# Mixing stage: query blocks in pairs from the middle outwards, alternating by groups of four heads

## The reference

```python
# A: memory branch (mLSTM), 16 chunks of 128 tokens, 4 heads; the state goes from chunk to chunk
(h, C, n, m) = mlstm(q, k, v, gates, chunk=128)        # a recurrence over the chunks
# B: sparse attention, 16 query blocks of 128 tokens, 8 query heads, 2 key heads (4 query heads share one)
_, sel = top_k(indexer_scores(iq, iw, ik, visible), 256)
yb = softmax(q @ k[sel].T * HD ** -0.5) @ v[sel]       # query t sees keys 0 .. t only
```

## Time and profile before

| | us |
|---|---|
| runs | 4074.53, 4076.52, 4077.44; median 4076.52 |
| span of the profiled execution | 4076.9 |
| TensorE busy | 3909.3 (96%) |
| VectorE busy | 2910.3 (71%) |
| GpSimd busy | 1670.9 (41%) |
| ScalarE busy | 1430.2 (35%) |
| mixing stage, first score matmul to last copy | 2255.0 to 3103.6 |

### The profile page before, as it was taken

One profiled execution on the slowest core, in us unless ns is written; L12 is line 12 of the kernel. 1 busy time (PEld: TensorE's weight loads), 2 busy tenths in 40 slices (PEclk: granted clock), 3 DMA queues, 4 the chain that ended last, 5 costly groups with the idle time before them and its releaser, 6 DMA issues. The chain is left out here.

```text
span 4076.9 us, 41822 instructions
## 1 busy us (share of the span) xinstructions
PE 3909.3 (96%) x14574; PEld 2311.2 (57%) x14574; DVE 2910.3 (71%) x3885; ACT 1430.2 (35%) x2616; POOL 1670.9 (41%) x1517
## 2 busy tenths in 40 slices
PE   7899999999999999999998799899999899999999
PEld 4555555563465556655665566555554688854444
DVE  4589989668999999999997555544543577753333
ACT  4411211155324443343331566545553322211111
POOL 0000036459786665566554232222202666552111
PEclk9999999999999999999999899999999899999999
DMA  5312222420111111211211643222232755541111
GB/s 217 90 53 65 64 83 84 141 89 36 59 66 64 63 60 62 69 62 68 68 63 58 179 110 103 66 84 64 78 97 73 214 168 168 169 143 60 41 57 46
DMA packets 290632, 367.34 MB, mean 90 GB/s; under 512 B 72223, under 2 KB 219187, under 8 KB 287734
## 3 DMA queue, kind: packets, MB, share of 16 engines
q1 hardware_dynamic: 250602, 249.50, 20.2%
q0 software_dynamic: 18704, 85.56, 5.7%
q10 hardware_dynamic: 21120, 29.66, 2.4%
HBM read 235.11 MB, written 128.23 MB: 89 GB/s over the span
## 5 line engine op out<-in xcount | busy, mean ns | idle before, releaser
L1274 DVE MAX8 best<-score 128x8 f32<-128x640 f32 (+13 forms) x448 | 639.6, 1428 | 60.4 <-POOL score L1235 45.4
L1276 DVE MATCH_REPLACE8 score<-best,score 128x640 f32<-128x640 f32 (+13 forms) x448 | 631.1, 1409 | 0.0
L1026 PE MATMUL pr<-xnT,w_row 128*128 128x347 f32 (+1 forms) x960 | 300.5, 459 | 0.0
L1176 POOL TENSOR_TENSOR kT<-kT 128x347 f32<-128x347 f32 (+1 forms) x240 | 194.5, 811 | 227.7 <-ACT kT L1096 221.3
L382 PE MATMUL pg<-xnT,wt 128*128 128x416 f32 x800 | 282.0, 515 | 0.0
L1642 PE MATMUL mix_slot<-mix_kT,mix_bq 128*128 128x512 f32 (+3 forms) x640 | 270.6, 539 | 5.9 <-DVE mix_mx L1921 5.0
L1026 PEld LDWEIGHTS pr<-xnT,w_row 128*128 128x128 f32 x960 | 178.2, 189 | 116.8 <-ACT kT L1096 19.3
L1697 PE MATMUL mix_po<-mix_probT,mix_v 128*128 128x512 f32 x544 | 240.3, 595 | 1.6 <-ACT mix_probT L1795 1.2
L1096 ACT COPY kT<-pr 128x347 f32<-128x347 f32 (+1 forms) x240 | 107.4, 449 | 350.1 <-PE pr L1026 337.4
L382 PEld LDWEIGHTS pg<-xnT,wt 128*128 128x128 f32 x800 | 152.7, 191 | 127.7 <-issue 127.7
L1921 DVE CUSTOM_DVE_ANT_0 early<-mix_slot,mix_mk 128x1024 f32<-128x1024 f32 (+7 forms) x86 | 84.8, 986 | 192.1 <-PE mix_pg L1651 131.8
(11 more groups left out here) (637 smaller groups left out, 8153.0 us busy)
## 6 DMA issues: line engine op xcount, KB each, us to landing
gt_scr<-kT SPq DMA_DIRECT2D x40, 694.0 KB, 3.3
out_gm<-gt_scr ACTq DMA_DIRECT2D x32, 520.0 KB
gt_scr<-kT SPq DMA_DIRECT2D x20, 692.0 KB, 4.3
wt<-in_w_in SPq DMA_DIRECT2D x22, 512.0 KB, 4.3
w0a<-in_w_in SPq DMA_DIRECT2D x11, 1024.0 KB, 5.2
w_row<-in_w_in SPq DMA_DIRECT2D x10, 1024.0 KB
qt_scr<-kT POOLq DMA_DIRECT2D x8, 1040.0 KB, 4.2
early<-ybt_scr SPq DMA_DIRECT2D x4, 2080.0 KB, 9.6
```

The source lines that it names most:

```text
L1026: ins = nc.tensor.matmul(pr[:, b, 0:w], lhs, rhs, start=k == 0, stop=k == 3)
L1176: nc.gpsimd.tensor_tensor(o[:, slot, :], o[:, slot, :], term, ALU.add).then_inc(added, 1)
L1274: nc.vector.max(best[:, :], sc).then_inc(top_step, 1)
L1276: nc.vector.match_replace(sc, best[:, :], sc, TAKEN).then_inc(top_step, 1)
```

## The change

The heads are walked through in another order. `BLOCK_ORDER` is 7, 8, 6, 9, 5, 10, 4, 11, 3, 12, 2, 13, 1, 14, 0, 15. Within a pair the two blocks alternate by groups of four heads: four heads of block 7, four of block 8, the other four of block 7, the other four of block 8, then blocks 6 and 9. The list keeps its form, and the memory branch and the sample's events keep their steps: M1 to Y of chunk t stand in steps 8(t-1) to 8(t-1)+5, which are now four heads of the smaller block and then two of the larger. All counts that were block times 8 plus head become the position in the new order. `FIRST_KEYS` is 8, so the first load of keys and values has eight tiles. `follow` now looks at the turning head (more than two groups of turns, blocks 8 to 15) and no longer at the scores.

```diff
 FIRST_SAMPLE_STEP = 12
-FIRST_KEYS = 4
+FIRST_KEYS = 8
+
+
+BLOCK_ORDER = [b for n in range(NB // 2) for b in (NB // 2 - 1 - n, NB // 2 + n)]
+GROUP_ORDER = [(b, kv) for n in range(NB // 2) for kv in range(KV) for b in BLOCK_ORDER[2 * n:2 * n + 2]]
+HEAD_ORDER = [(b, BH // KV * kv + x) for b, kv in GROUP_ORDER for x in range(BH // KV)]
+BLOCK_AT = {b: n for n, b in enumerate(BLOCK_ORDER)}
+GROUP_AT = {g: n for n, g in enumerate(GROUP_ORDER)}
+HEAD_AT = {h: n for n, h in enumerate(HEAD_ORDER)}
 
...
-    heads = [(i, hd) for i in range(NB) for hd in range(BH)]
+    heads = HEAD_ORDER
...
-    events = [(m, 0) for m in ("M1", "M2", "M3", "Q", "M4", "Y")] + [("S", 0, hd) for hd in range(AHEAD)]
-    events += [("E", 0, hd) for hd in range(AHEAD - 1)] + [("N", 0, hd) for hd in range(AHEAD - 2)]
+    events = [(m, 0) for m in ("M1", "M2", "M3", "Q", "M4", "Y")] + [("S", *h) for h in heads[:AHEAD]]
+    events += [("E", *h) for h in heads[:AHEAD - 1]] + [("N", *h) for h in heads[:AHEAD - 2]]
     for n, (i, hd) in enumerate(heads):
+        t, at = n // BH + 1, n % BH
...
-        if hd == 3 and i + 1 < NB:
-            events.append(("Q", i + 1))
-        if hd % 4 == 3:
+        if at == 3 and t < NB:
+            events.append(("Q", t))
+        if at % 4 == 3:
             events.append(("O", i, hd // 4))
-        if i + 1 < NB and hd in (0, 1, 2, 4, 5):
-            events.append(({0: "M1", 1: "M2", 2: "M3", 4: "M4", 5: "Y"}[hd], i + 1))
+        if t < NB and at in (0, 1, 2, 4, 5):
+            events.append(({0: "M1", 1: "M2", 2: "M3", 4: "M4", 5: "Y"}[at], t))
     return events
...
-            n = 2 * i + kv
+            n = GROUP_AT[i, kv]
...
-            def load_a(i):
-                p, rows = i % 2, slice(i * P, (i + 1) * P)
-                if i >= 2:
-                    after_slot(sp, ("S", i - 2, BH - 1, key_pieces(i - 2) - 1))
+            def load_a(n):
+                i, p = BLOCK_ORDER[n], n % 2
+                rows = slice(i * P, (i + 1) * P)
+                if n >= 2:
+                    before = BLOCK_ORDER[n - 2]
+                    after_slot(sp, ("S", before, BH - 1, key_pieces(before) - 1))
                 for dst, src in ((bq[p][:, :, :], d["qt"][T_BQ:T_BK, :, rows].rearrange("t p q -> p t q")),
                                  (mk[p][:, 0:(i + 1) * P], d["mask"][i, :, 0:(i + 1) * P])):
                     sp.dma_start(dst, src).then_inc(a_loaded[p], 16)
...
-                p = i % 2
+                n = BLOCK_AT[i]
+                p = n % 2
                 if hd == 0 and q == 0:
-                    pe.wait_ge(a_loaded[p], 32 * (i // 2 + 1))
+                    pe.wait_ge(a_loaded[p], 32 * (n // 2 + 1))
                     pe.wait_ge(k_resident[i >= FIRST_KEYS], 16)
...
             for a, b in zip(long, long[1:]):
-                if a[0] == "T" and b[0] == "S" and key_pieces(b[1]) == 2:
+                if a[0] == "T" and b[0] == "S" and key_groups(a[1]) > 2:
                     follow[b] = a
...
-                    if 2 * i + kv:
-                        pe.wait_ge(oT_ready, 2 * i + kv)
+                    if GROUP_AT[i, kv]:
+                        pe.wait_ge(oT_ready, GROUP_AT[i, kv])
...
-                if hd % 4 == 0 and 2 * i + hd // 4:
-                    act.wait_ge(o_mm, 2 * i + hd // 4)
+                if hd % 4 == 0 and GROUP_AT[i, hd // 4]:
+                    act.wait_ge(o_mm, GROUP_AT[i, hd // 4])
...
-                    hd = e[2]
-                    act.wait_ge(nbias_ready, BH * i + hd + 1)
-                    if i:
-                        act.wait_ge(inverse, BH * (i - 1) + hd + 1)
-                    nc.scalar.activation(prob[(BH * i + hd) % AHEAD][:, 0:(i + 1) * P], prob[(BH * i + hd) % AHEAD][:, 0:(i + 1) * P], ACT.Exp,
-                                         scale=SCALE, bias=mx[:, (BH * i + hd) % AHEAD, 1:2], accum_out=sums[:, hd:hd + 1]).then_inc(p_ready, 1)
+                    n = HEAD_AT[i, e[2]]
+                    act.wait_ge(nbias_ready, n + 1)
+                    if n >= BH:
+                        act.wait_ge(inverse, n - BH + 1)
+                    scores = prob[n % AHEAD][:, 0:(i + 1) * P]
+                    nc.scalar.activation(scores, scores, ACT.Exp, scale=SCALE, bias=mx[:, n % AHEAD, 1:2],
+                                         accum_out=sums[:, n % BH:n % BH + 1]).then_inc(p_ready, 1)
...
-                    hd = e[2]
-                    b = (BH * i + hd) % AHEAD
+                    n = HEAD_AT[i, e[2]]
+                    b, block_no = n % AHEAD, BLOCK_AT[i]
                     for q, (lo, width) in enumerate(pieces((i + 1) * P)):
                         s = slot_filled(dve, (*e, q))
                         if q == 0:
-                            dve.wait_ge(a_loaded[p], 32 * (i // 2 + 1))
-                            if BH * i + hd >= AHEAD:
-                                j, hp = divmod(BH * i + hd - AHEAD, BH)
+                            dve.wait_ge(a_loaded[block_no % 2], 32 * (block_no // 2 + 1))
+                            if n >= AHEAD:
+                                j, hp = HEAD_ORDER[n - AHEAD]
                                 dve.wait_ge(turned, bank_no[("T", j, hp, key_groups(j) - 1)] + 1)
...
```

More of the change, by code:

```diff
@@ L1551, in _ @@
             sp.wait_ge(oT_ready, 2 * NB)
-            store_oT(sp, NB - 1, 1)
+            store_oT(sp, *GROUP_ORDER[-1])
             sp.wait_ge(last_out, 3)
@@ L1608, in _ @@
                     pool.dma_start(d["y"][rows, 0:D].rearrange("q (h e) -> q h e", h=AH), ya[:, :, :]).then_inc(ya_stored, 16)
-                elif e[0] == "O" and 2 * i + e[2] + 1 < 2 * NB:
-                    pool.wait_ge(oT_ready, 2 * i + e[2] + 1)
+                elif e[0] == "O" and GROUP_AT[i, e[2]] + 1 < len(GROUP_ORDER):
+                    pool.wait_ge(oT_ready, GROUP_AT[i, e[2]] + 1)
                     store_oT(pool, i, e[2])
@@ L1647, in turn_group @@
                 if q == 0:
-                    pe.wait_ge(normed, BH * i + hd + 1)
+                    pe.wait_ge(normed, HEAD_AT[i, hd] + 1)
                 s = take_bank((*e, q))
                 for t in range(4 * q, min(4 * q + 4, i + 1)):
-                    ins = turn(pg[:, s, (t % 4) * P:(t % 4 + 1) * P], prob[(BH * i + hd) % AHEAD][:, t * P:(t + 1) * P], c["ident"][:, :])
+                    ins = turn(pg[:, s, (t % 4) * P:(t % 4 + 1) * P], prob[HEAD_AT[i, hd] % AHEAD][:, t * P:(t + 1) * P], c["ident"][:, :])
                 ins.then_inc(turned, 1)
@@ L1825, in _ @@
                     kv = e[2]
-                    act.wait_ge(o_mm, 2 * i + kv + 1)
-                    n = 2 * i + kv
+                    n = GROUP_AT[i, kv]
+                    act.wait_ge(o_mm, n + 1)
                     if n >= 2:
@@ L1921, in _ @@
                         nc.vector.tensor_tensor_reduce(out=prob[b][:, lo:lo + width], in0=slot[:, s, 0:width],
-                                                       in1=mk[p][:, lo:lo + width], scale=1.0,
+                                                       in1=mk[block_no % 2][:, lo:lo + width], scale=1.0,
                                                        scalar=mx[:, b, 0:1] if q else TAKEN, op0=ALU.add, op1=ALU.max,
@@ L1925, in _ @@
                     after_slot(dve, (*e, q))
-                    if BH * i + hd >= AHEAD:
-                        dve.wait_ge(p_ready, BH * i + hd - AHEAD + 1)
+                    if n >= AHEAD:
+                        dve.wait_ge(p_ready, n - AHEAD + 1)
                     nc.vector.tensor_scalar(mx[:, b, 1:2], mx[:, b, 0:1], -SCALE, None, ALU.mult).then_inc(nbias_ready, 1)
                 elif kind == "N":
-                    n = BH * i + e[2]
-                    b = n % AHEAD
+                    n = HEAD_AT[i, e[2]]
+                    b, at = n % AHEAD, slice(n % BH, n % BH + 1)
                     dve.wait_ge(p_ready, n + 1)
-                    nc.vector.reciprocal(rsum[:, e[2]:e[2] + 1], sums[:, e[2]:e[2] + 1]).then_inc(inverse, 1)
+                    nc.vector.reciprocal(rsum[:, at], sums[:, at]).then_inc(inverse, 1)
                     dve.wait_ge(inverse, n + 1)
-                    nc.vector.tensor_scalar(prob[b][:, 0:(i + 1) * P], prob[b][:, 0:(i + 1) * P], rsum[:, e[2]:e[2] + 1], None,
+                    nc.vector.tensor_scalar(prob[b][:, 0:(i + 1) * P], prob[b][:, 0:(i + 1) * P], rsum[:, at], None,
                                             ALU.mult).then_inc(normed, 1)
```

## The result

The changed kernel takes 4094.65 us (median of 6 runs, 4089.7 to 4117.2), the kernel before in the same comparison 4076.98 (6 runs, 4074.5 to 4084.1): a ratio of 1.005, 95% interval 1.0033 to 1.0066, slower by 17.7 us. The profiled execution has a span of 4088.1. Its windows of the mixing stage, cut where a group of value matmuls ends (columns as in the earlier trace rows): the whole stage, the first half of a pair, the second, the seventh, the last but one and the last.

The account below looks back on a forecast made before the run. The mixing stage was taken as bound by TensorE, with 78.8 us lost to idle time and half clock. The terms sum to 95.4 in place of that, +16.6 us, so 4093; own range 4082 to 4104, with rivals 4064 to 4112.

Parts of the forecast that it names:

- (1): M2, M3 and M4 wait for a score slot behind long heads' scores, three waits per half: 27.6 us, before 18.4.
- (3): M1's chain of copy, decay matrix and product holds up the reduction in pairs with short blocks 3 to 0: 6.4 us.
- (2): Second group of turns waits 0.80 us for ScalarE's copy of memory keys, pairs with short blocks 7 to 4: 6.4 us.
- (4): Long heads followed by short scores: turns and value matmuls wait for ScalarE and VectorE, 40 us including the stage's tail.
- rival A: Faster: ScalarE and VectorE have the next long head ready, so 25 us of waits are hidden: 4068, chance 0.15.
- (5): The sample's softmax falls on four long heads of the fifth pair, with steps of 3 us instead of 8: 2 us.
- (6): Stage start: late first reduction and half clock until about 2278 lose 13 us in place of block 0's 22.
- (7): SyncE's loads keep their place, GpSimd's stores and gathers their steps, the next phase's load comes early enough: nothing.
- C: Slower still: ScalarE sets the pace in the four outer pairs, 3 us more per half, with late keys: 4121, chance 0.12.
- D: The clock is halved after the turns in the eight outer halves, 6 us each, 48 in all: 4141, chance 0.03.

Follow-up runs that it names:

- e4: The changed kernel with Y moved from the sixth to the eighth head of each half, behind the value matmuls' event: 4094.19 us, ratio 1.0048 to the kernel before.
- e1: The kernel before with only its first load of keys and values enlarged from 4 tiles to 8, old block order: 4079.49 us, ratio 1.0003.
- e2: The changed kernel's block order, but all eight heads of a block in a row: 4085.34 us, ratio 1.0023 to the kernel before.
- e5: The changed kernel with M2, M3 and M4 whole and ahead of the scores: 4097.72 us, ratio 1.005 to the kernel before.

## Why the prediction was right, and where it wasn't

The forecast was +16.6 us, and the medians differ by 17.7, the profiled stages by 15.2. By its steps:

- (1), slot waits: right. M3 and M4 wait 8.4 + 9.7 = 18.1 us where the term has 18.4. In the first half M2, M3 and M4 wait 1.43, 1.20 and about 1.3, and M1 doesn't.
- (3), M1's chain: 6.4 was the term. M2's 16.1 us are 6.9 more than the 9.2 that (1) has for it, and with the 3.0 of the second score pieces that makes 9.9. The chain as it was walked through is there in about its size, 5.6 without what follows: in the second half of the fifth pair, with short block 3, M2's 1.29 is 0.85 over the slot's 0.44, where 0.7 to 0.9 was expected. What the walk didn't have is VectorE's normalisation behind the product, which GpSimd's step makes longer in four first halves, by 4.3 us in all; that is more than the 3.5 by which the term was too small, and it starts with the second pair and not with block 3. The trace of the kernel before had shown such a normalisation (2.07 us at 2356.82, beside GpSimd's step from 2357.33). The half clock behind two of these waits, 2 x 3.4 x 0.5 = 3.4 us, was not in the sum either.
- (2), bank wait: 6.4 of 6.4.
- (4), long heads: 40 against 12.0 + 22.9 less the 2.4 at the start, 32.5. The waits for the last copy were right in the outer pairs and somewhat high in the inner ones (0.4 to 0.9 each, 12.0 for sixteen). What was mis-sized is above all the walk of the two outermost pairs: waits of this kind are 2.3 and 2.4 us in the halves of the seventh, where it has 3.8, and 3.0 in the first of the last, where it has 5.0. The walk put the state updates, two normalisations and Y one behind the other; e4 shows Y's share, 6.0 us of idle time in one execution, and rival A's cover is there in part.
- (5), sample softmax: 2 was the term. The halves of the fifth pair have 2.2 and 2.7 us of such waits where (4) has 1.9 each, 1.1 more in all and inside the 32.5; how much of that is the softmax isn't shown.
- (6), start: the idle part is 4.8 us, and the clock is back at 2262.8, not 2278, so half clock takes 1.7; 6.5 in place of 13.
- (7), loads and queues: nothing, as said. No wait for keys stands in the changed kernel's trace, and e1 confirms the load for the old order. In e2 GpSimd's queue was the cost, so "keep their steps" protects only where the steps keep their length.
- Also not in the sum: a wait costs more than its gap (last section). Busy time is up 3.9 us although half clock in the stage fell from 8.4 to 5.1, so 7.2 at full clock. There are 109 waits of over 0.1 us in place of 81; 28 at 0.16 make 4.5 of the 7.2, the rest isn't accounted for.

So the mechanisms of (1), (2) and most of (3) were right, but that the sum came within 1.5 us was luck, by errors against each other: 40 + 2 + 13 was 16 us too much for (4), (5) and (6), and 14.5 was missing: 3.2 in (1) and (3) together, 3.4 of clock behind waits, 7.2 of busy time, 0.7 of small gaps. The 5 us by which the other executions are longer than the profiled one were missing too. The rivals: A's hidden waits exist, 7.5 us of 25. C's slow ScalarE is not there; it is busy for 29.54 of 52.10 us in the last but one half, and the turns wait 0.6 to 0.9 us for its copies in each of halves 11 to 15. D's half clock behind the turns isn't there either. The stretch 3003 to 3010 holds the 30 turns of two long heads, sixteen small products of the sample and four short score matmuls, and the value matmuls behind it run at full clock:

```profile
3003.00:3010.00 7.00, 5.51 (x50) 4.07 (x50) 4.67 (x22) 6.14 (x13) 1.15 (x1) 1.00 0.30 119
3010.00:3023.30 13.30, 13.17 (x34) 5.78 (x34) 0.47 (x3) 0.44 (x4) 0.00 (x0) 1.00 0.00 0
```

By the rule of the Trainium skill, "TensorE: Matmul & The Clock Gate", section "Part 4: PE-mode transpose", these turns would not have counted as activity; the trace disagrees over these 7 us as over those of the earlier trace rows. Where the clock fell in this stage, at the start and in the two places above, a wait of 1.97 us or more had come just before.

## What to carry to other kernels

A chain that crosses engines (here TensorE, ScalarE, VectorE, then TensorE) should start ahead of a long run of work that needs none of them, and can fill the gap ahead of that run as well: this one move was worth 19 us in one order and 34 in the other, more than any order of blocks. Before an order is judged, such a fixed cost of each turn-over has to be out, for it grows or shrinks with the order and hides what the order does. And where one list orders all engines, a step moved earlier for one is moved ahead of other steps on all of them. And a step that takes 0.5 us alone can take 2 us beside another engine's, so it is worth looking for its longest case in the trace before a chain is added up.

## What the runs showed of the hardware

A wait costs TensorE more than its gap. In the changed kernel (timeline, from 2593.14), four turns of a head are followed by the fifth after a gap of 0.80:

```profile
2592.70 0.60 PE L1776 MATMUL mix_pg<-ident,sm_C 128*128 128x128 f32 x4
2593.14 0.60 PE L1663 MATMUL mix_pg<-ident,early 128*128 128x128 f32 x4
2594.54 0.33 PE L1663 MATMUL mix_pg<-ident,early 128*128 128x128 f32 x1 [0.80 <-ACT sm_C L1817]
```

Four turns back to back move the next start by 0.44 (2592.70 to 2593.14), here it moves by 1.40: 0.96 is lost for a gap of 0.80. The 0.16, by my reading, is the end of the last matmul, which otherwise lies under the next, and is counted as busy.

A step of VectorE and one of GpSimd can hold each other up. In all fourteen traces the mixing stage's normalisation on VectorE is over 0.25 us longer than its like only where GpSimd's masking step (L1586 in the changed kernel) overlaps it: 1.80 us for 0.55, 2.06 for 0.49. Where VectorE's began first it can be the other way: in e5 GpSimd's step at 2288.13 takes 1.74 us, 1.26 to 1.29 elsewhere in that trace, and the normalisation of 2287.93 its usual 0.82. Not every overlap costs that much.

The clock fell to 0.50 after waits of 1.97 and 2.72 us, but the length of a wait doesn't settle it. In the same trace it stayed at 1.00 after waits of 1.67, 1.82 and even 2.37:

```profile
2264.66 1.10 PE L1663 MATMUL mix_pg<-ident,early 128*128 128x128 f32 x8 [2.37 <-DVE early L1948]
```

and in the kernel with M1 early it fell after this same wait (at 2268.15) and after one of 1.70 (at 3066.87). The kernel with M1 early has 6 us between its executions, the changed one 27. By my reading short stretches of half clock, which come in some executions and not in others, make a kernel with many waits of 2 us both slower and harder to measure.
